# Mask of the nearest keys added to the position bias on GpSimd, in a ring of four tiles

## The reference

```python
def dsa_attention(q, k, v, iq, ik, iw, bias_table, k_sel):
    ...
        _, sel = lax.top_k(score, k_sel)
        valid = (sel // CHUNK) <= (qpos[None, :, None] // CHUNK)
        kg = gather(k, sel)
        vg = gather(v, sel)
        s = jnp.einsum('bqhd,bqkhd->bhqk', qb, kg).astype(jnp.float32) * scale
        rel = sel - qpos[None, :, None]
        bias = jnp.transpose(bias_table[t5_bucket(rel)], (0, 3, 1, 2)).astype(jnp.float32)
        s = jnp.where(valid[:, None], s + bias, -jnp.inf)
        p = jax.nn.softmax(s, axis=-1)
        return jnp.einsum('bhqk,bqkhd->bqhd', p.astype(v.dtype), vg)
```

## Time and profile before

| | us |
|---|---|
| median of 3 runs (lowest, highest) | 797.35 (795.86, 798.42) |
| the profiled execution | 797.5 |
| its span | 795.3 |

### The profile page before, as it was taken

How to read it: one execution, slowest core, us unless ns; L and a number is a source line. 1 busy time by engine, 2 the same in 40 slices (tenths; PEclk the granted TensorE clock), 3 DMA queues, 4 the chain that set the end, 5 groups by cost and what they waited for, 6 DMA issues and landing times.

```text
span 795.3 us, 11730 instructions
## 1 busy us (share of the span) xinstructions
PE 758.3 (95%) x4161; PEld 634.8 (80%) x4161; DVE 613.6 (77%) x1300; ACT 304.8 (38%) x677; POOL 319.2 (40%) x383
## 2 busy tenths in 40 slices
PE   4999999999999989999999999998999999899996
PEld 3765888888888878889888888886888888888885
DVE  3738999999998959878699999995767667534343
ACT  5437222031315546667520312106545455422221
POOL 5320122224534958761355553557996500300000
PEclk9999999999999989999999999999999999999998
DMA  7242111111102020021112111200311100121231
GB/s 277 55 120 66 40 45 48 54 43 51 53 15 53 0 54 19 10 79 44 43 50 54 40 53 54 67 14 26 107 41 67 28 2 1 47 100 67 92 106 53
DMA packets 24560, 44.54 MB, mean 56 GB/s; under 512 B 3076, under 2 KB 9912, under 8 KB 24376
## 3 DMA queue, kind: packets, MB, share of 16 engines
q1 hardware_dynamic: 24504, 43.81, 18.6%
HBM read 35.40 MB, written 6.57 MB: 53 GB/s over the span
## 4 chain that ended last, share of the span: by engine, by line
PE 64%; DVE 22%; POOL 5%; issue 3%; ACT 3%; DMA 2%; SPq 0%; DVEq 0%; ACTq 0%; POOLq 0%
PE psum L1100 20%; PE psum L1266 11%; PE psum L1205 10%; DVE score L1431 9%; DVE top L1426 9%; PE psum L1187 5%; PE psum L1162 4%; PE psum L1165 4%; PE psum L1000 3%; PE psum L1028 3%; PE psum L1044 1%; DMA k_high_twice<-k_high_twice 1%; ACT probsT_B L867 1%; DMA xs<-in_x 1%; PE psum L949 1%
## 5 line engine op out<-in xcount | busy, mean ns | idle before, releaser
L558 POOL TENSOR_TENSOR w_lo<-w_raw,w_hi 128x512 fp32r<-128x512 f32 x60 | 77.9, 1300 | 226.8 <-ACT w_hi L713 226.4
L1431 DVE MATCH_REPLACE8 score<-top,score 128x768 f32<-128x768 f32 (+5 forms) x176 | 157.3, 906 | 0.0
L1426 DVE MAX8 top<-score 128x8 f32<-128x768 f32 (+5 forms) x176 | 148.2, 909 | 1.1
L713 ACT ACTIVATE w_hi<-w_raw 128x512 fp32r<-128x512 f32 x60 | 37.7, 630 | 221.2 <-PE psum L1100 208.8
L856 ACT ACTIVATE probs<-psum,small 128x384 f32<-128x384 f32 (+7 forms) x128 | 94.9, 742 | 52.7 <-DVE small L1450 36.0
L1100 PE MATMUL psum<-w_hi,big_hi 128*128 128x512 f32 x256 | 99.6, 389 | 0.0
L1100 PE MATMUL psum<-w_lo,big_hi 128*128 128x512 f32 x256 | 99.6, 389 | 0.0
L1100 PE MATMUL psum<-w_hi,big_lo 128*128 128x512 f32 x256 | 99.6, 389 | 0.0
L1205 PE MATMUL psum<-v,probsT_B 128*128 128x64 f32 x576 | 74.8, 274 | 3.7 <-ACT probsT_B L867 2.6
L1205 PEld LDWEIGHTS psum<-v,probsT_B 128*128 128x128 f32 x576 | 70.4, 192 | 7.9 <-ACT probsT_B L867 3.6
L1100 PE MATMUL psum<-big_hi,w_hi 128*128 128x512 f32 x192 | 74.8, 390 | 0.0
(11 more groups left out here) (172 smaller groups left out, 1574.6 us busy)
## 6 DMA issues: line engine op xcount, KB each, us to landing
w_raw<-in_w_in SPq DMA_DIRECT2D x62, 256.0 KB, 2.6
xs<-in_x SPq DMA_DIRECT2D x8, 512.0 KB, 6.4
k_high_twice<-k_high_twice SPq DMA_DIRECT2D x16, 256.0 KB, 3.8
xres<-in_x SPq DMA_DIRECT2D x8, 512.0 KB, 3.5
out_y<-y_out SPq DMA_DIRECT2D x16, 256.0 KB, 2.1
w_tail<-in_w_out SPq DMA_DIRECT2D x10, 256.0 KB, 2.6
bias_scratch<-bias_row SPq DMA_DIRECT2D x1, 2304.0 KB
bias<-bias_scratch SPq DMA_DIRECT2D x12, 128.0 KB, 3.2
```

The source lines that it names most:

```text
L558: pool.tensor_tensor(lo[:, 0:cols], w_staged(n)[:, 0:cols], hi[:, 0:cols].bitcast(f32), ALU.subtract).then_inc(w_lo_made, 1)
L713: act.activation(w_parts(n)[0][:, 0:cols], w_staged(n)[:, 0:cols], ACT.Copy).then_inc(w_hi_made, 1)
L1426: ins = dve.max(top8[:, i - SEL0, :], sc)
L1431: ins = dve.match_replace(sc, top8[:, i - SEL0, :], sc, TAKEN)
```

## The change

The mask products of the second attention go. In their place GpSimd adds the mask of a unit's last 256 keys to its head's bias (`near`), into one of four tiles `near_bias`, which lie where `biasA_hi` of the first attention was, and `soften` adds such a tile in place of `bias`, once it is made (`near_made`). There is one for each of the 48 masked units. A tile is written again once the unit four masked units earlier is softened (`max_ready`). GpSimd's work is ordered anew around it, by step: the two tiles of the next step, then in a block's first four steps one part of the next block's split, in the three after two chunks of output weights each.

```diff
-    biasA_hi, _ = place("biasA_hi", [P, A_HEADS, BAND], f32r)
+    biasA_hi, biasA_hi_at = place("biasA_hi", [P, A_HEADS, BAND], f32r)
+    near_bias, _ = place("near_bias", [P, 4, BAND], f32, at=biasA_hi_at)
...
+        near_units = [2 * s + m for s in range(STEPS) for m in range(2) if place_of(1, s)[1] >= SEL0]
+        near_of = {u: k for k, u in enumerate(near_units)}
...
-            for b in range(1, BLOCKS):
-                for j in range(4):
-                    split_part(1, b, j)
-                if b < BLOCKS - 1:
-                    for n in range(CHUNKS + 6 * (b - 1), CHUNKS + 6 * b):
-                        w_out_parts(n)
-                    wait_split(pool, CHUNKS + 6 * b - 1)
+            def near(s, m):
+
+                if 2 * s + m not in near_of:
+                    return
+                k = near_of[2 * s + m]
+                b, i = place_of(1, s)
+                if k >= 4:
+                    pool.wait_ge(max_ready, 2 * STEPS + near_units[k - 4] + 1)
+                end = score_off[i] + P * (i + 1)
+                pool.tensor_tensor(near_bias[:, k % 4, :], bias[:, A_HEADS + 2 * b + m, :], mask[:, end - BAND:end],
+                                   ALU.add).then_inc(near_made, 1)
+
+            pool.wait_ge(mask_made, TILES - SEL0)
+            near(0, 0)
+            near(0, 1)
+            for s in range(STEPS):
+                if s + 1 < STEPS:
+                    near(s + 1, 0)
+                    near(s + 1, 1)
+                if s < 3 * TILES and s % TILES < 4:
+                    pool.wait_ge(near_made, sum(u < 2 * s + 4 for u in near_units))
+                    split_part(1, s // TILES + 1, s % TILES)
+                elif s < 2 * TILES and s % TILES < 7:
+                    first = CHUNKS + 6 * (s // TILES) + 2 * (s % TILES - 4)
+                    w_out_parts(first)
+                    w_out_parts(first + 1)
+                    if s % TILES == 6:
+                        wait_split(pool, first + 1)
             pool.wait_ge(s_ready, 4 * STEPS)
...
-                masked = ph == 1 and i >= SEL0
...
-                if masked:
-                    pe.wait_ge(mask_made, TILES - SEL0)
...
-                    banded = (masked or ph == 0) and near < c + w
+                    banded = ph == 0 and near < c + w
...
-                    elif banded:
-                        mk = mask[:, score_off[i] + near:score_off[i] + c + w]
-                        ins = pe.matmul(score_of(u, near, c + w), identb[:, :], mk, start=False, stop=True)
...
-                dve.tensor_tensor_reduce(out=o, in0=o, in1=bias[:, h, BAND - w:BAND], scale=1.0,
+                added = bias[:, h, BAND - w:BAND]
+                if u - 2 * STEPS in near_of:
+                    k = near_of[u - 2 * STEPS]
+                    dve.wait_ge(near_made, k + 1)
+                    added = near_bias[:, k % 4, :]
+                dve.tensor_tensor_reduce(out=o, in0=o, in1=added, scale=1.0,
```

More of the change, by code:

```diff
@@ L243, in build @@
         mask_made = sem("mask_made")
+        near_made = sem("near_made")
         s_ready = sem("s_ready")
@@ L1163, in scores @@
                     near = max(c, length - BAND)
-                    banded = (masked or ph == 0) and near < c + w
+                    banded = ph == 0 and near < c + w
                     ins = pe.matmul(o, q[:, qt], low[:, c:c + w], start=False, stop=not banded)
-                    if banded and ph == 0:
+                    if banded:
                         bs = slice(BAND - length + near, BAND - length + c + w)
```

## The result

| | before | after |
|---|---|---|
| median, us (runs, lowest to highest) | 797.35 (7, 795.86 to 799.25) | 801.0 (7, 798.67 to 802.46) |
| the profiled execution | 797.5 | 800.47 |
| its span | 795.3 | 798.6 |

The ratio is 1.0043, 95% interval 1.0026 to 1.006: slower by 0.4%, and inside the stated range. The profiled executions differ by 3.0 us.

A forecast was written before the change was run, and what follows sets the result against it. GpSimd's queue was to become the bound of two blocks and part of the third: 797.5 + 6.8 us late at (21, 0) - 1.8 won back after it = 802.5 us, range 798.0 to 807.5.

The forecast's parts named there:

- The mechanism: Second attention: GpSimd needs 39.3 us a block against TensorE's 35.1, so late tiles stall `soften`; 10.2 us of new stalls.
- The price of an add: GpSimd's 128 x 256 add: 0.70 us, interpolated between measured adds of 128 and 512 columns; bounds 0.42 and 0.97.
- a rival: GpSimd's adds are cheap, below 0.46 us, one operand being half as wide: faster, 793.8 us at 0.42; chance 0.15.
- the fixed part: 0.15 us in each GpSimd add beside 2.1 ns a column; without it 256 columns would be 0.56 us.
- some 3 us a block to give: GpSimd's room early in the second attention: busy 33.27 us in the period from 563.95, of a 36.55 us block.
- The removal: TensorE's queue in the second attention loses 56 mask products, 5.9 us, of which 5.2 us counted as won.
- The rival of the clock: New stalls cost TensorE its granted clock, 3.4 us lost, giving 805.9 us; chance 0.06 together with another rival.
- the prediction's own signs of being wrong: Adds well below 0.6 us, no `soften` waits for GpSimd, all periods near 35.1, or granted clock below 1.00 in this stage.

The follow-up runs named there:

- the removal alone: Kernel before without the 56 mask products and nothing in their place: 793.88 us against 796.79, ratio 0.9957.
- The run with the tiles unused: GpSimd's queue with all 48 adds as changed, but mask products kept and `soften` adding the plain bias without waiting for tiles: 796.87 us against 796.79, ratio 0.9998.
- the doubled adds: Changed kernel with each of the first 31 adds made a second time behind a wait for the first: 825.39 us, ratio 1.0356.
- the late chunks: Changed kernel with the twelve output-weight chunks moved to steps 23 to 28 and SyncE's key copies put before the fourth chunk's load: 793.87 us, ratio 0.9961.
- The fp32 run: Changed kernel with the add's second operand taken from the other head's fp32 bias in place of the bf16 mask: 804.12 us, ratio 1.009.
- the two with the chunks late: Changed kernel with output-weight chunks moved to steps 23 to 28, 793.87 us; the same with each block's fourth split part in step 5, 794.18 us.

## Why the prediction was right

**The mechanism** was right step by step: GpSimd's queue is longer than TensorE's in the blocks 0 and 1, `soften` waits at (5, 0), (6, 0), (13, 0), (14, 0) and (21, 0) and nowhere else, the waits at (5, 0), (13, 0) and (21, 0) go through VectorE's move to TensorE, and the last period is free again. The delays at (6, 0) and (14, 0) were carried on as well: from (6, 0) `soften` was ready for (13, 0) after 31.76 us, and in the run with the removal alone after 31.86 (564.53 to 596.39). Their way over ScalarE is not shown by itself, for TensorE ran slowly there and has no new idle time. GpSimd had no wait up to 644.43. The periods are 38.5 and 35.45 us for 39.3 and 35.1, the waits of `soften` 7.2 us for some 10. The run with the tiles unused shows that it is the wait, the doubled adds that it is carried whole, and the late chunks that the load is what makes it.

**The price of an add** is the term that was mis-sized: 0.70 us, measured 0.64. Worked through the same sum, 31 x 0.06 = 1.9 us less at (21, 0), 4.9 instead of 6.8, and measured 4.75; the sum then ends at 800.6. The fp32 run shows the interpolation exact for what it was made of; the bf16 operand, whose discount I had given only to a rival, takes off 9%. The rule that the prediction cites with the price from the Trainium skill ("GPSIMD Engine Reference", section "Elementwise — side-by-side cycle accounting"), a floor for each element of a two-input add, holds in this trace to within that 9%: an operand of half the width did not come at half the price. That the fixed part belongs in (0.56 without it) was right. Two smaller slips changed nothing: an add of 0.61 us gives 799.7 by the sum, not 799.9; and the "some 3 us a block to give" were read from a stretch that holds parts of two blocks' work, while the prediction's own prices make it 19.0 + 6 x 1.95 = 30.7 us a block, and its sum went by these.

**The removal** was counted with 5.2 us of 5.9; the profile of the run without them gives 4.1, its executions 3.4 (2.3 to 4.5). One of the places where a product that goes is not won was seen, the two in the iterations of the steps 7 and 2, 0.12 us each, were not. In the changed kernel this term is worth less than it looks: before (21, 0), where the queue rules, it only lengthens the stalls (7.2 us in all, against 10.2 predicted). What is really won back is what lies behind (21, 0), 4.75 - 3.65 = 1.1 us up to (29, 0), which starts at 675.68 against 672.03 one period after 635.48 in the earlier trace rows, and 0.35 more up to the end of the span, against 1.8 predicted.

**The rival of the clock** was not expected, since a wait of 2.3 us had been followed by no fall, and this was wrong; a clock below 1.00 in this stage was one of the prediction's own signs of being wrong, and it is 0.96 in two periods. After TensorE's waits for (5, 0) and (13, 0), 1.51 and 1.64 us, the granted clock fell to half; after that for (21, 0), 1.71 us, it did not. What the rival added to the time, 3.4 us, did not come. The windows of the changed kernel:

```profile
562.00:564.00 2.00, 0.53 (x5) 0.39 (x4) 0.84 (x4) 0.25 (x1) 1.92 (x4) 1.00 0.30 68
564.00:566.00 2.00, 1.96 (x10) 1.68 (x11) 1.68 (x8) 1.49 (x4) 1.92 (x3) 0.88 0.79 207
566.00:568.00 2.00, 2.00 (x9) 1.81 (x8) 0.78 (x2) 0.62 (x2) 1.92 (x3) 0.50 0.35 127
568.00:570.00 2.00, 2.00 (x16) 2.00 (x15) 1.64 (x6) 1.09 (x2) 1.92 (x4) 0.76 0.41 135
```

2 x (0.12 + 0.50 + 0.24) = 1.7 us of TensorE's time were lost here, and none of it reached the end. `soften` (6, 0) had to wait for its tile until 568.32 in any case, and TensorE, instead of waiting behind it, ran slowly: its `weigh` at 570.70 waits 0.40 us for ScalarE, as the one at 568.59 did before the change. After (13, 0) the fall lay earlier (0.77, 0.50 and 0.88 from 602 to 608) and shortened the wait at (14, 0), 0.82 us where (6, 0) has 1.54; yet both units start equally far behind the one before, 5.16 and 5.14 us, for GpSimd's queue sets that distance. A loss on one engine is free as long as another's queue sets the next meeting. Behind the last such meeting it is not free, as the fp32 run shows (1.44 us) and the doubled adds (2.1).

## What to carry to other kernels

- Before giving work to an engine that is 40% busy, add up its queue between two points where others wait for it, and compare it with the period of the bound engine there. Here 38.5 us stood against 35.4 in two blocks, though over the whole span GpSimd was busy for only 44%.
- What counts is the work queued ahead of the thing waited for. Work nobody waits for (here the output weights) belongs behind the last such hand-over: the same change with that one move, and the loads on SyncE put in its order, is 0.4% faster than before, not 0.4% slower.
- When a step is moved, follow the other queues that wait for it: a later split part held a copy on SyncE, and the loads behind that copy then cost GpSimd 3 us twice.

## What the runs showed of the hardware that I had not expected

- GpSimd's add of 128 x 256 takes 0.64 us from one start to the next with one bf16 operand, and 0.70 with both in fp32 (2.55 and 2.79 us for four).
- A TensorE wait of 1.5 us can be followed by half the granted clock (1.2 of 2.4 GHz): in the changed kernel 0.88, 0.50 and 0.76 in the three stretches of 2 us from 564. In the same kernel a wait of 1.7 us was followed by none (1.00 from 640 to 648).
- At the start of the second attention TensorE waits 2.2 to 2.3 us in every profile. In the two with the mask products (the kernel before and the one with the tiles unused) the granted clock stayed at 1.00 behind it. It fell to 0.50 between 542 and 549 in the profiles of all eight experiments without them, but not in that of the changed kernel. The executions' mean clocks point the same way: 0.992 or lower in 23 of the 31 of the three kernels without products that have at most one stall (the removal alone, and the two with the chunks late), in 10 of the 30 of the kernel before beside them, and in none of the 12 with the tiles unused. Why the products matter for it was not tried.
- Such a fall cost nothing when it ended by 547 (the removal alone), and 1.5 to 2.8 us at (5, 0) when it lasted to 552 or 556 (the two kernels with the chunks late).
